# First dense feed-forward pass written out with one wait per load, and the experts' first five loads moved from the end of the output projection to the merge of the branches

## What is computed

```python
def reference(...):
    for l in range(DEPTH):
        h = rmsnorm(x, g_mix[l])
        ...
        merged = (gates[:, :, 0] * (o_fox @ p_fox[l])
                  + gates[:, :, 1] * (o_dsa @ p_dsa[l])
                  + gates[:, :, 2] * (o_rwkv @ p_rwkv[l]))
        x = x + merged @ w_out[l]
        h2 = rmsnorm(x, g_ffn[l])
        if l % 2 == 0:
            y = swiglu(h2, ffn_w_gate[l // 2], ffn_w_up[l // 2], ffn_w_down[l // 2])
        else:
            y = moe_ffn(h2, router_w[l // 2], router_b[l // 2],
                        moe_w_gate[l // 2], moe_w_up[l // 2], moe_w_down[l // 2])
        x = x + y
    return rmsnorm(x, g_final)
```

## Time and profile before

| | us |
|---|---|
| median of 3 executions (lowest, highest) | 1916.46 (1913.86, 1917.31) |
| the profiled execution's own time | 1917.06 |
| its span, first to last instruction | 1915.0 |
| TensorE busy with matmuls in it | 1842.4 |
| mean granted TensorE clock, of full speed | 0.985 |
| DMA queue of all weight loads, share of 16 engines' span | 63.3% |

### The profile page before, as it was taken

One profiled execution on the slowest core, in us unless ns is written; L12 is line 12 of the kernel. 1 busy time (PEld: TensorE's weight loads), 2 busy tenths in 40 slices (PEclk: granted clock), 3 DMA queues, 4 the chain that ended last, 5 costly groups with the idle time before them and its releaser, 6 DMA issues.

```text
span 1915.0 us, 42076 instructions
## 1 busy us (share of the span) xinstructions
PE 1842.4 (96%) x19380; PEld 1198.9 (63%) x19380; DVE 395.0 (21%) x817; ACT 237.8 (12%) x466; POOL 49.7 (3%) x98
## 2 busy tenths in 40 slices
PE   6999999999999999999799999999999999999996
PEld 5788888788887787888634445354453534435344
DVE  1356223100001356223310101101011010101102
ACT  1324111100001325111100000000000000000001
POOL 3000200000000000200000000000000000000000
PEclk9999999999999999999799999999999999999998
DMA  6432212434334432212689999999999999999970
GB/s 186 154 132 89 84 52 88 176 131 173 134 110 137 142 132 89 79 56 89 265 337 370 404 375 393 362 386 383 385 404 363 384 378 377 403 375 385 371 296 23
DMA packets 122838, 462.08 MB, mean 241 GB/s; under 512 B 9566, under 2 KB 20496, under 8 KB 106288
## 3 DMA queue, kind: packets, MB, share of 16 engines
q1 hardware_dynamic: 122672, 459.46, 63.3%
HBM read 458.39 MB, written 1.05 MB: 240 GB/s over the span
## 4 chain that ended last, share of the span: by engine, by line
PE 96%; DVE 2%; ACT 1%; issue 1%; DMA 1%; SPq 0%; DVEq 0%; ACTq 0%
PE bank L1006 30%; PE bank L383 25%; PE bank L1023 15%; PE bank L885 4%; PE bank L675 3%; PE bank L845 3%; PE bank L716 2%; PE bank L832 1%; PE bank L960 1%; PE bank L970 1%; PE bank L422 1%; PE bank L369 1%; PE bank L377 0%; DMA slot<-in_ffn_w_gate 0%; PE bank L759 0%
## 5 line engine op out<-in xcount | busy, mean ns | idle before, releaser
L1006 PE MATMUL bank<-slot,xg 128*32 128x512 f32 (+1 forms) x6144 | 587.1, 539 | 0.0
L383 PE MATMUL bank<-h,slot 128*128 128x256 f32 x2176 | 486.4, 383 | 7.5 <-ACT rel L1442 5.3
L383 PEld LDWEIGHTS bank<-h,slot 128*128 128x128 f32 x2176 | 413.5, 191 | 70.4 <-issue 13.6
L1006 PEld LDWEIGHTS bank<-slot,xg 128*32 128x32 f32 x6144 | 204.9, 110 | 371.6 <-issue 364.6
L1023 PE MATMUL bank<-slot,aT 128*32 128x256 f32 x5376 | 293.0, 379 | 0.0
L1023 PEld LDWEIGHTS bank<-slot,aT 128*32 128x32 f32 x5376 | 174.7, 110 | 118.8 <-issue 6.2
L2103 DVE TENSOR_TENSOR av<-gs,bank 128x512 f32<-128x512 f32 (+1 forms) x48 | 29.8, 621 | 577.0 <-PE bank L1006 575.1
L885 PE MATMUL bank<-hid,slot 128*128 128x256 f32 x352 | 77.0, 379 | 0.9 <-DVE hid L1971 0.9
L885 PEld LDWEIGHTS bank<-hid,slot 128*128 128x128 f32 x352 | 66.8, 190 | 10.3 <-issue 1.2
L1581 ACT ACTIVATE gs<-bank 128x512 f32<-128x512 f32 (+1 forms) x48 | 25.2, 543 | 284.6 <-PE bank L1006 284.5
L845 PE MATMUL bank<-sq,slot 128*128 128x256 f32 x256 | 56.2, 379 | 0.0
(11 more groups left out here) (398 smaller groups left out, 1165.7 us busy)
## 6 DMA issues: line engine op xcount, KB each, us to landing
slot<-in_moe_w_gate SPq DMA_DIRECT2D x32, 2048.0 KB, 12.4
slot<-in_moe_w_up SPq DMA_DIRECT2D x32, 2048.0 KB, 17.4
slot<-in_moe_w_down SPq DMA_DIRECT2D x32, 2048.0 KB, 10.7
slot<-in_moe_w_gate SPq DMA_DIRECT2D x32, 1536.0 KB, 8.6
slot<-in_moe_w_up SPq DMA_DIRECT2D x32, 1536.0 KB, 11.0
slot<-in_moe_w_down SPq DMA_DIRECT2D x32, 1536.0 KB, 8.6
slot<-in_w_in SPq DMA_DIRECT2D x20, 2048.0 KB, 8.0
slot<-in_ffn_w_gate SPq DMA_DIRECT2D x5, 2048.0 KB, 7.8
```

The source lines that it names most:

```text
L383: ins = mm(o, w[:, k, c:c + n], rhs[:, k, :], start=k == 0, stop=k == nk - 1)
L1006: ins = mm(o.rearrange("s (b c) -> s b c", c=32), xg[:, g, k, :], strip(w[:, kk, :], p), start=k == 0, stop=k == KD - 1)
```

## The change

1. The dense part's first pass is written out in front of the loop, which now runs passes 1 to 4. The four clearing matmuls are gone. In the written-out pass the first product into each of banks 4 to 7 carries the start flag instead, and `bank_full` of these banks is raised by the down products.
2. SP's first three dense loads are written out too. Each waits for its own slot alone.
3. The experts' ring starts at slot 3: load n goes to slot (n + 3) % 8 (`ring_at`). The first five loads, into slots 3 to 7, wait for the last `merged` of layer 1. The sixth waits for the four additions to `x`, as the first did before.

```diff
+        def ring_at(n):
+            return (n + NS) % NSE
...
                                     ins = mm(v2(banks[4 + m // 2])[:, m % 2, :], w[:, k, m * P:(m + 1) * P],
-                                             hid[:, k, :], start=first and k == 0, stop=last and k == nf - 1,
+                                             hid[:, k, :], start=first and k == 0 and m % 2 == 0, stop=last and k == nf - 1,
...
+                                if first and g == 0 and m % 2:
+                                    ins.then_inc(bank_full[4 + m // 2], 1)
...
-                    for bi in range(4, 8):
-                        mm(banks[bi][:, :], cst[:, 0:1].broadcast_to([P, P]), cst[:, 0:1].broadcast_to([P, 512]),
-                           start=True, stop=False, skip_group_check=True).then_inc(bank_full[bi], 1)
                     need(pe, "h_ready", KD * 2)
-                    with pe.Fori(0, DI) as i:
+                    dense(0, 4, True, False)
+                    with pe.Fori(1, DI) as i:
                         dense(i, 4, False, False)
...
                 def slot(n):
-                    si, r = n % NSE, n // NSE
+                    si, r = ring_at(n), n // NSE
...
-                    for si in sl3:
-                        sm, v = before[(si, ld[si])]
-                        sp.wait_ge(sm, v)
...
-                    with sp.Fori(0, DI) as i:
+                    for si, t_, src in ((0, c3(slots[sl3[0]], KD, 512), wg[:, :, 0:512]),
+                                        (1, c3(slots[sl3[1]], KD, 512), wu[:, :, 0:512]),
+                                        (2, c3(slots[sl3[2]], 4, D), wd[:, 0:4, :])):
+                        sm, v = before[(sl3[si], ld[sl3[si]])]
+                        sp.wait_ge(sm, v)
+                        sp.dma_start(t_, src).then_inc(slot_full[sl3[si]], 16)
+                    with sp.Fori(1, DI) as i:
...
-            for g in range(4):
-                need_sb(sp, f"1xo{g}")
...
-                        sp.dma_start(dst, src.rearrange("o p k n -> (o p) k n")).then_inc(slot_full[n % NSE], 16)
+                        sp.dma_start(dst, src.rearrange("o p k n -> (o p) k n")).then_inc(slot_full[ring_at(n)], 16)
...
+            need(sp, "merged", 8)
+
             def first_free(n):
+                if n == NSE - NS:
+                    for g in range(4):
+                        need_sb(sp, f"1xo{g}")
                 if n >= NSE:
                     sp.wait_ge(S["slots_used"], n - NSE + 1)
```

More of the change, by code:

```diff
@@ L1231, in expert @@
                             src = t_[bass.ds(e, 1), :, r0:r0 + nb_, :]
-                            dst = c3(slots[n % NSE], nb_, D)
+                            dst = c3(slots[ring_at(n)], nb_, D)
                         else:
                             src = t_[bass.ds(e, 1), :, 2 * q:2 * q + 2, c0:c0 + 4 * width]
-                            dst = c3(slots[n % NSE], 2, 4 * width)
+                            dst = c3(slots[ring_at(n)], 2, 4 * width)
                         free(n)
-                        sp.dma_start(dst, src.rearrange("o p k n -> (o p) k n")).then_inc(slot_full[n % NSE], 16)
+                        sp.dma_start(dst, src.rearrange("o p k n -> (o p) k n")).then_inc(slot_full[ring_at(n)], 16)
                         n += 1
+            need(sp, "merged", 8)
             def first_free(n):
+                if n == NSE - NS:
+                    for g in range(4):
+                        need_sb(sp, f"1xo{g}")
                 if n >= NSE:
```

## The result

| | before | after |
|---|---|---|
| median, us (lowest, highest) | 1916.88 (1913.86, 1918.73) | 1944.87 (1939.98, 1949.26) |
| ratio | | 1.0150, 95% interval 1.0132 to 1.0169 |
| profiled execution's own time | 1917.06 | 1940.59 |
| its span | 1915.0 | 1938.5 |

The changed kernel is 1.5% slower, 28 us. The forecast was 1915.9 with a range up to 1919.0. It was wrong.

What follows compares the result with a forecast made beforehand. TensorE bounds the kernel (96% of the chain), so loads count only where it waits. Profiled 1917.06 - 0.76 (dense start) + 0.23 (clock) = 1916.53, less 0.60 for the median: 1915.9 us, range 1913.0 to 1919.0.

Steps and rivals of the forecast that it cites:

- The pass written out: Dense part's first pass: same 192 products, loop branch moves to the seam of passes 0 and 1; cost taken as nothing.
- the sum: Whole kernel: profiled 1917.06 - 0.76 + 0.23 = 1916.53 us, less 0.60 for the median, 1915.9 us.
- The rival on fetches: Dense loop's entry: branch stalls TensorE for an instruction fetch, 3.5 us slower; chance 0.04 above 0.2%, 0.03 below.
- The dense start: Dense part's first gate product: waits only for h, not its load, and starts at 358.73 instead of 359.49; 0.76 us gained.
- The clock at the dense part: First dense products without clearing matmuls: begin at half clock, losing 2.17 us where 1.94 is lost now; 0.23 us lost.
- the rival in which they keep the clock up: Dense part: clearing matmuls prevent the clock's fall in other executions, so the change is 1.2 us slower, 1917.7; chance 0.22.
- The experts' five loads: Experts' first loads, issued at 896.76 instead of 925.48 beside the output projection: gain 0, contention cost 0.
- The items' stretches: Item loop: the 480 products of an item stay at 46.52 us.

Runs made afterwards that it cites:

- without the mark: Changed kernel with its item loop's head at slot 140 and the hint ahead of the loop's backward branch removed: 1962.63 us, ratio 1.0233.
- the moved kernel before: Kernel before with one instruction added that puts its item loop's head at slot 214 of its fetch block: 1944.29 us, ratio 1.0152.

## Why the prediction was wrong

**The step that failed** is "The pass written out": "TensorE executes the same 192 products in it. What moves is the branch into the loop", and from it "I take nothing, the row of the same operation at the same place." As far as it goes it was right, with no gap at 402.30. But a step that adds code moves more than a branch into a loop. It moves everything behind it by 371 instructions, and the item loop, 600 us later, has a branch whose cover depends on its place. This term was missing from the sum, and it measured +27.9 us.

**The rival on fetches** had the right mechanism and the wrong branch. It priced one entry (at most 3.5 us, chance 0.04) and took "backward branches without a gap" as evidence against it. Two kinds of branches stand behind that. The row at 402.88 is from the dense loop, and that loop's code stays in the engine: from 445 to 565, across two of its backward branches, no packet of q8 begins, in either kernel. It is no row for a branch whose target must be fetched. The item loop's code is fetched anew each time, and that its branches had no gap was evidence for a good place, not for a free branch. The same rival with seven branches, each with the stall of 2.8 us now measured and the clock's fall of 1.9, would have been 7 x (2.8 + 1.9) = 33 us, less the 5 us that the kernel before already lost to its own place: 28.

**The dense start**: 0.76 us forecast, 359.49 to 358.73. It came to 358.78, 0.71. Of that, h itself was 0.26 early, as the whole execution was from its first products on (30.46 against 30.72 in the two chains), and TensorE started 0.36 behind h, not 0.04. That leaves 0.45 for the edit.

**The clock at the dense part**: it fell before the products began (0.51 in 356 to 357, 0.50 until 362), as forecast. The first block took 29.87, forecast 29.6 to 29.8, so 0.30 was lost where I said 0.23. The dense edits net 0.15 us in this pair where the sum had 0.53. The fall wasn't prevented by the clearing matmuls in any of the five kernels that have them. The first block took 29.31 to 29.58 us in their traces, and 29.84 to 29.98 in seven without them. So the rival in which they keep the clock up is out as far as these traces go.

```profile
356.00:357.00 1.00, 0.00 (x0) 0.00 (x0) 1.00 (x4) 0.00 (x0) 0.00 (x0) 0.51 0.99 397
357.00:362.00 5.00, 3.22 (x8) 2.63 (x9) 1.41 (x4) 0.00 (x0) 0.00 (x0) 0.50 0.04 15
```

**The experts' five loads**: 0 forecast; 0.9996 measured alone.

**The items' stretches** of 46.52 us stayed as they were, as forecast. I had taken that row for the item; it holds 480 products from the middle of one, and the branch is outside it.

## What to carry to other kernels

Code added anywhere ahead of a loop whose body is fetched anew in every turn can change what its backward branch costs; here one line that moves only the loop's head put the changed kernel anywhere between 0.9965 and 1.033 of the kernel before. After an edit to an engine's stream, look at the waits with no releaser right behind each backward branch, and at the q8 packets beside them, before judging the edit itself. Compare two versions at the same place of the loop's head, and choose the place with room on both sides: the branch late in its block (slot 178 hid everything, 137 left up to 0.5 us), and more than 100 instructions left behind the head (116 hid everything, about 86 didn't).

## What the runs showed of the hardware

- Instructions that TensorE fetches come 16 KB a packet, and run 2.5 to 2.8 us after the packet's start, under a DMA share of about 1.0 and 400 GB/s. A backward branch without the mark stopped TensorE for 5.1 us in the mean. The packet of the block behind the head's began 2.2 to 3.0 us after the head's first product.
- The Trainium skill, "Runtime: NRT & Kernel Launch", section "Instruction fetch mechanics", calls the crossing of a block "mostly hidden". The crossings inside an item were: no idle time stands in its 480 products. At the branch and in the block behind the loop's head they were not: in the badly placed kernels they stopped TensorE for 2.2 to 4.1 us each.
- After each of the seven gaps of the changed kernel the granted clock was at 1.2 GHz for a while, which cost 1.7 to 1.9 us of the next 96 products (12.04 to 12.20, less 10.30). After the gaps of the moved kernel before (2.2 us) it fell in five items and not in two: the granted clock was 1.00 from 1075.84 to 1084, behind the first gap, and 0.62 in 1792 to 1796, behind the last, and its items are 118.1 us or 119.7 to 120.1.
- An early mark alone doesn't hide a branch: 399 instructions ahead gave the same gap of 3 us as 255, at the changed kernel's own place.
